# Seven products in place of eight for a part of the second feed-forward matrix, in an fp32 kernel of one core

## The reference

```python
def swiglu(x, w_in, w_out):
    gu = x @ w_in
    g, u = gu[..., :D_FF], gu[..., D_FF:]
    return (jax.nn.silu(g) * u) @ w_out
...
x = layer_norm(ALPHA * x + 0.5 * swiglu(x, ffn_w_in[l, 0], ffn_w_out[l, 0]), ln_g[l, 0], ln_b[l, 0])
...
    h = h + (jax.nn.silu(g_ff) * u_ff) @ w_ffn_out[l]
```

## Time and profile before

| | |
|---|---|
| time, median of 3 runs | 3251.34 us (3250.98 to 3256.97) |
| profiled execution | 3251.48 us, of which span from first to last instruction 3249.7 us |
| TensorE matmuls | 24214, busy 3157.5 us (97%) |
| VectorE | busy 2143.2 us (66%) |
| ScalarE | busy 1535.2 us (47%) |
| HBM read | 325.69 MB, 101 GB/s over the span |
| granted TensorE clock, mean | 0.994 |

### The profile page before, as it was taken

One profiled execution on the slowest core, in us unless ns is written; L12 is line 12 of the kernel. 1 busy time (PEld: TensorE's weight loads), 2 busy tenths in 40 slices (PEclk: granted clock), 3 DMA queues, 4 the chain that ended last, 5 costly groups with the idle time before them and its releaser, 6 DMA issues. The chain is left out here.

```text
span 3249.7 us, 58922 instructions
## 1 busy us (share of the span) xinstructions
PE 3157.5 (97%) x24214; PEld 2863.2 (88%) x24214; DVE 2143.2 (66%) x3383; ACT 1535.2 (47%) x2651; POOL 137.5 (4%) x144
## 2 busy tenths in 40 slices
PE   9999999999999999999999988999999989999999
PEld 9998998999889988779998877879998867789997
DVE  7875544788577856448875766557874665667863
ACT  4553444355435543644553544444554444444553
POOL 0000111000000001000000100000000000000000
PEclk9999999999999999999999999999999999999999
DMA  4343222234323332112433221113332211123332
GB/s 180 143 141 110 95 72 90 76 136 148 117 88 127 134 121 93 53 66 88 143 134 123 86 72 60 37 63 117 131 142 97 99 66 53 41 83 119 141 126 72
DMA packets 104523, 331.73 MB, mean 102 GB/s; under 512 B 11264, under 2 KB 16640, under 8 KB 104256
## 3 DMA queue, kind: packets, MB, share of 16 engines
q1 hardware_dynamic: 104256, 327.96, 28.7%
HBM read 325.69 MB, written 2.23 MB: 101 GB/s over the span
## 5 line engine op out<-in xcount | busy, mean ns | idle before, releaser
L222 DVE TENSOR_TENSOR wlo<-raw,whi 128x1024 fp32r<-128x1024 f32 x319 | 387.7, 1224 | 433.3 <-ACT whi L214 432.6
L214 ACT ACTIVATE whi<-raw 128x1024 fp32r<-128x1024 f32 x319 | 334.2, 1055 | 386.4 <-PE ps L379 333.5
L803 PE MATMUL ps<-tz,whi 128*128 128x256 f32 x1728 | 477.6, 276 | 3.4 <-ACT tmp L975 3.4
L804 PE MATMUL ps<-tz,whi 128*128 128x256 f32 x1728 | 477.1, 276 | 0.0
L805 PE MATMUL ps<-tz,wlo 128*128 128x256 f32 x1728 | 477.1, 276 | 0.0
L241 PE MATMUL ps<-xh,whi 128*128 128x256 f32 x1424 | 410.3, 288 | 18.4 <-DVE wlo L222 11.1
L377 PE MATMUL ps<-whi,tz 128*128 128x512 f32 x1056 | 412.1, 390 | 0.0
L379 PE MATMUL ps<-whi,tz 128*128 128x512 f32 x1056 | 411.0, 389 | 0.0
L378 PE MATMUL ps<-wlo,tz 128*128 128x512 f32 x1056 | 410.9, 389 | 0.0
L243 PE MATMUL ps<-xh,wlo 128*128 128x256 f32 x1424 | 397.9, 279 | 0.0
L242 PE MATMUL ps<-xl,whi 128*128 128x256 f32 x1424 | 397.7, 279 | 0.0
(11 more groups left out here) (348 smaller groups left out, 6509.2 us busy)
## 6 DMA issues: line engine op xcount, KB each, us to landing
raw<-in_w SPq DMA_DIRECT2D x535, 512.0 KB, 3.7
fb<-in_w SPq DMA_DIRECT2D x108, 256.0 KB, 2.5
rows<-in_row SPq DMA_DIRECT2D x15, 512.0 KB, 4.6
xr<-in_xt SPq DMA_DIRECT2D x4, 512.0 KB, 6.6
xr<-in_x SPq DMA_DIRECT2D x1, 2048.0 KB, 7.4
mn<-bounds SPq DMA_DIRECT2D x8, 256.0 KB, 4.6
out<-tmp SPq DMA_DIRECT2D x4, 256.0 KB, 3.5
out<-rows SPq DMA_DIRECT2D x4, 256.0 KB, 2.3
```

Source lines behind the costliest of these rows:

```text
L214: a.activation(self.whi[u % NW][:, :], self.raw[u % NRAW][:, :], COPY).then_inc(*self.up("whi", u))
L222: v.tensor_tensor(self.wlo[u % NW][:, :], self.raw[u % NRAW][:, :], f32(self.whi[u % NW][:, :]), SUB).then_inc(*self.up("wlo", u))
L803: t.matmul(out, fh[:, sl], xh[:, k, :], start=first and k == 0, stop=False, skip_group_check=not first)
L804: t.matmul(out, fh[:, sl], xl[:, k, :], start=False, stop=False, skip_group_check=not first)
```

## The change

In each feed-forward layer row blocks 6 to 13 (`PRE` = 6, `POST` = 14) of the second matrix are multiplied by the seven-product scheme. The quarters are: row blocks 6 to 9 and 10 to 13, the two 256-column halves of a column half, and the even and the odd token tiles. Products are made for each pair p of token tiles (0, 1 and 2, 3).

The order on TensorE becomes (`out_t`): row blocks 0 to 5 of half 0, then of half 1; seven products for half 0; row blocks 14 to 21 of half 0; seven products for half 1; row blocks 14 to 21 of half 1. The sums over row blocks 0 to 5 are taken out of PSUM and added to the residual (`part_v`), and the rest is added at the end by `add_v`. A row block's matmuls have 256 columns in place of 512 (`rows_t`). The activations of a row block are split once: high parts into `tz`, low parts into `hr`, which takes the place of `hf` in memory. The forms of the activations (`HAND`, `hand_a`, `hand_sum_v`, `hand_low_v`) are made once, in the place of `xh` and `xl` (`xx`), `tz` and `hr`. The forms of the weights (`out_sum_v`, `out_hi_a`, `out_lo_v`) are made for each half: four units of quarters give seven forms, which take the buffers `whi` and `wlo` in turn. Two of the sums lie in `fb` and `es`, two are made in place in `raw`. The stream of weights is reordered to match. The places in memory are shifted by padding.

```diff
-LINE = 16
+LINE = 32
+PRE = 6
+POST = 14
+PAIRS = (POST - PRE) // 2
+OUT_ORDER = (1, 5, 2, 6, 3, 7, 4)
...
+        self.v0 = u0 + 2 * KF
+        self.nm = nm.start(self.v0, KF)
+        for h in range(2):
+            v = self.first(h)
+            for i in range(4):
+                c.freed[v + 4 + i] = "prod", s, "out", h, OUT_ORDER[4 + i if i < 3 else 3], 1
+                c.read[v + i] = "flo", s, "out", h, (0, 5, 6, 4)[i]
...
+    def first(self, h):
+        return self.v0 + PRE + h * (KF - PRE) // 2
...
+    def out_from(self, h, f):
+
+        one, two = self.fb[:, :], self.es[:, 0:2, :].rearrange("p a n -> p (a n)")
+        return (self.out_raw(h, 0), one, self.out_raw(h, 2), two, self.out_raw(h, 3), self.out_raw(h, 1), self.out_raw(h, 2))[f]
...
+    def rows_t(self, t, h, k, i, first=False, last=False, event=None):
...
+        for e in range(2):
+            cs = slice(e * HT, e * HT + HT)
+            t.matmul(b[:, cs], hh[:, sl], wh[:, cs], start=first and e == 0, stop=False, skip_group_check=k >= POST)
+            t.matmul(b[:, cs], hh[:, sl], wl[:, cs], start=False, stop=False, skip_group_check=k >= POST)
+            ins = t.matmul(b[:, cs], hl[:, sl], wh[:, cs], start=False, stop=last and e == 1, skip_group_check=k >= POST)
...
+    def out_product(self, t, h, n, p, f):
...
+        for q in range(PAIRS):
+            x, cs = 2 * q + p, slice(q * HT, q * HT + HT)
+            t.matmul(out, fh[:, x, :], wh[:, cs], start=first and q == 0, stop=False, skip_group_check=not first)
+            if n == 1 and q == 0:
+                t.matmul(self.abe(h, p, r)[:, HT:T], fh[:, x, :], wh[:, cs], start=False, stop=False, skip_group_check=True)
+            t.matmul(out, fh[:, x, :], wl[:, cs], start=False, stop=False, skip_group_check=not first)
+            ins = t.matmul(out, fl[:, x, :], wh[:, cs], start=False, stop=q == PAIRS - 1, skip_group_check=not first)
...
+    def seven_out_t(self, t, h):
+        c, s, n = self.c, self.s, self.nm.n
+        for f, x in enumerate(OUT_ORDER):
+            if x == 4:
+                t.wait_ge(*c.at("g2", s, "out", h, 0))
+                for k in (POST, POST + 1):
+                    if k == POST:
+                        t.wait_ge(*c.at("wlo", self.unit_of(h, k)))
+                    t.wait_ge(*c.at("hl", s, k))
+                    self.rows_t(t, h, k, 0)
+            t.wait_ge(*c.at("flo", s, "out", h, f))
...
+            for p in range(2):
+                if x == 1 and h == 0:
+                    t.wait_ge(*c.at("part", n, 0, 2 * p))
+                elif x == 5:
+                    t.wait_ge(*(c.at("res", n, 0, 2 * p) if h else c.at("part", n, 1, 2 * p)))
...
+                self.out_product(t, h, x, p, f)
...
+    def out_hi_a(self, a, h, f):
+
+        c, s, u = self.c, self.s, self.first(h)
+        a.wait_ge(*(c.at("gemm", "unit", u - NW + f) if f < NW else c.at("prod", s, "out", h, OUT_ORDER[f - NW], 1)))
...
+    def out_a(self, a):
...
+        for h in range(2):
+            for f in range(4):
+                self.out_hi_a(a, h, f)
+                if h == 0 and f == 1:
+                    self.split_a(a, POST + 2, POST + 3)
+            self.out_seed_a(a, h, 0)
+            self.out_seed_a(a, h, 1)
+            self.out_hi_a(a, h, 4)
+            self.out_e5_a(a, h, 0)
+            self.out_e5_a(a, h, 1)
+            self.out_hi_a(a, h, 5)
+            self.out_hi_a(a, h, 6)
+            self.out_u2c_a(a, h, 0)
+            self.out_u2c_a(a, h, 1)
+            if h == 0:
+                self.split_a(a, POST + 4, POST + 5)
...
+            u = self.first(h) + 4
+            c.one_hi(a, u + 3)
+            c.one_hi(a, u)
+            c.one_hi(a, u + 1)
+            if h == 0:
+                self.split_a(a, POST + 6, POST + 7)
+            c.one_hi(a, u + 2)
...
+    def out_v(self, v):
...
+        c.one_lo(v, units[3])
+        c.one_lo(v, units[2])
+        self.hand_sum_v(v, "S1")
+        self.hand_sum_v(v, "S3")
+        self.hand_sum_v(v, "S2")
+        c.one_lo(v, units[4])
+        self.hand_sum_v(v, "S4")
+        self.hand_low_v(v, "A11", "A12")
+        c.one_lo(v, units[5])
+        self.hand_low_v(v, "S1")
+        for i in range(4):
+            self.part_v(v, 0, i)
+        self.out_sum_v(v, 0, 1)
+        self.out_lo_v(v, 0, 0)
+        self.hand_low_v(v, "S2")
+        self.out_sum_v(v, 0, 2)
+        self.out_lo_v(v, 0, 1)
+        self.hand_low_v(v, "S4")
+        self.out_sum_v(v, 0, 3)
+        self.out_lo_v(v, 0, 2)
+        self.out_sum_v(v, 0, 4)
+        self.hand_low_v(v, "S3", "A22")
+        for i in (0, 2, 1, 3):
+            self.part_v(v, 1, i)
+        for h in range(2):
+            self.out_lo_v(v, h, 3)
+            if h == 0:
+                self.split_v(v, POST, POST + 1)
+            self.out_lo_v(v, h, 4)
+            if h == 0:
+                self.split_v(v, POST + 2, POST + 3)
+            self.out_lo_v(v, h, 5)
+            self.out_lo_v(v, h, 6)
+            u = self.first(h) + 4
+            if h == 0:
+                self.split_v(v, POST + 4, POST + 5)
+            c.one_lo(v, u + 3)
+            self.out_g2_v(v, h, 0)
+            self.out_g2_v(v, h, 1)
+            c.one_lo(v, u)
+            self.out_u2_v(v, h, 0)
+            self.out_u2_v(v, h, 1)
+            c.one_lo(v, u + 1)
...
+            c.one_lo(v, u + 2)
```

More of the change, by code:

```diff
@@ L210, in hi, with one_hi @@
             u = self.nhi
[L211 to L214, removed]
+            self.one_hi(a, u)
             self.nhi += 1
+    def one_hi(self, a, u):
+        a.wait_ge(*self.at(f"raw{u % NRAW}", u))
+        if u >= NW:
+            a.wait_ge(*self.at(*self.freed.get(u, ("gemm", "unit", u - NW))))
+        a.activation(self.whi[u % NW][:, :], self.raw[u % NRAW][:, :], COPY).then_inc(*self.up("whi", u))
     def lo(self, v, upto):
@@ L329, in __init__, with start @@
         self.banks = (first, 4 - first)
-    def start(self, u0, k, feed=None):
-        self.u0, self.k, self.feed = u0, k, feed
+    def start(self, u0, k):
+        self.u0, self.k = u0, k
         self.end = u0 + k
@@ L683, in scalar @@
             c.hi(a, u + AHEAD)
-            if self.feed:
-                self.feed.split_a(a, 2 * (u - u0) + 4)
             if u0 + K // 2 < u <= u0 + K // 2 + 4:
                 self.square_a(a, 0, u - u0 - K // 2 - 1)
[L688 to L691, removed]
-        if not self.kind:
-            for i in range(4):
-                self.copy_a(a, 0, i)
         c.hi(a, self.end - 1)
@@ new lines, in out_lo_v, with part_v @@
+    def out_lo_v(self, v, h, f):
+        c, s = self.c, self.s
+        hi, lo = self.out_form(h, f)
+        v.wait_ge(*c.at("fhi", s, "out", h, f))
+        v.tensor_tensor(lo[:, :], self.out_from(h, f), f32(hi[:, :]), SUB).then_inc(*c.up("flo", s, "out", h, f))
+    def part_v(self, v, h, i):
+        c, nm = self.c, self.nm
+        v.wait_ge(*c.at("gemm", "part", nm.n, h, i))
+        if nm.n == 0 and h == i == 0:
+            v.wait_ge(*c.at("xrin"))
+        x = c.xr[:, i, 4 * P * h:4 * P * h + 4 * P]
+        v.scalar_tensor_tensor(out=x, in0=nm.bank(h, i), scalar=nm.by, in1=x, op0=MULT, op1=ADD).then_inc(*c.up("part", nm.n, h, i))
@@ new lines, in out_u2_v @@
+    def out_u2_v(self, v, h, p):
+        c, s = self.c, self.s
+        v.wait_ge(*c.at("prod", s, "out", h, 7, p))
+        v.wait_ge(*c.at("e5", s, "out", h, p))
+        b = self.abe(h, p, 1)
+        v.tensor_tensor(b[:, HT:T], b[:, 0:HT], c.tmp[p][:, HT:T], ADD).then_inc(*c.up("u2", s, "out", h, p))
+    def out_a(self, a):
+        c, v0 = self.c, self.v0
+        units = [self.unit_of(h, k) for h in range(2) for k in range(0, PRE, 2)]
+        self.split_a(a, 4, 5)
+        c.one_hi(a, units[3])
+        c.one_hi(a, units[2])
+        self.hand_a(a, "A11")
+        c.one_hi(a, units[4])
+        self.hand_a(a, "A12")
+        self.hand_a(a, "A22")
+        self.hand_a(a, "S1")
+        c.one_hi(a, units[5])
+        self.hand_a(a, "S3")
+        self.hand_a(a, "S2")
+        self.hand_a(a, "S4")
+        self.split_a(a, POST, POST + 1)
+        for h in range(2):
[14 more added lines that the diff above has]
+                self.split_a(a, POST + 4, POST + 5)
+            else:
+                for i in range(4):
+                    self.nm.square_a(a, 0, i)
+            u = self.first(h) + 4
[5 more added lines that the diff above has]
+            c.one_hi(a, u + 2)
+        c.nhi = self.nm.end
+        self.nm.finish_a(a)
```

321 lines of the change are left out of this document (269 added, 52 removed).

## The result

The changed kernel takes **3318.5 us** (median of 4 executions, 3304.5 to 3325.75) against 3251.2 us for the kernel before (4 executions, 3248.1 to 3257.0): ratio **1.020**, 95% interval 1.0162 to 1.0238. The forecast was 3291 us with a range of 3262 to 3312. The direction was right, the size was not: the kernel lost 67 us where 40 were forecast.

A forecast was written before the change was run, and what follows sets the result against it. The count of matmul columns on TensorE was taken to set the time in the rewritten stretch. 3251.3 - 29.9 (columns) + 51.0 (waits) + 18.6 (clock) = 3291 us, range 3262 to 3312.

The forecast's parts named there:

- Columns removed, -29.9 us: Second matrix, first feed-forward layers: 1012 units of 256 columns against 1056, 4.99 us a layer saved, 29.9 in all.
- Waits of the fetches, +51: TensorE waits after product 7 and before product 5 for late weights and sums: 8.5 us a layer, before the columns' gain.
- The landing, taken as 4.4 us: Time for the late weight unit u+3, fetched behind another, to arrive: 4.4 us, against 3.0 for a single fetch.
- The wait of 0.8 us before product 5: First half: product 5 waits for the second half's first `part` on VectorE, 0.8 us a layer.
- Clock, +18.6: The two TensorE pauses a layer lower the granted clock behind them, 1.7 us each time: 3.1 us a layer.
- The chance: Probability that a TensorE pause is followed by the lower clock: 0.95 for 4.2 us, 0.85 for 3.4 us.
- Two at 113.3 ns are one at 226.7 ns, so I take nothing: Second matrix: halving matmuls from 512 to 256 columns costs no time.
- The fixed cost per matmul: Skill page's 2.5 ns per matmul: 484 more matmuls a layer, estimated 1.2 us, 7 in all; not used.
- The one with 117.5 ns: Rival: second-matrix products and narrow rows run at 117.5 ns, 14 us more, 3305 us; chance 0.12 shared with longer low clock.
- The clock stays low for longer: Rival: 3.4 us lost at each TensorE pause, 41 us, giving 3313 us; chance 0.12 shared with slow narrow matmuls.
- the case that held them: Outcome class of slow narrow matmuls or longer low clock, 3303 to 3320 us, chance 0.12.
- The covered fetch: Rival: unit u+3 is in its buffer when ScalarE comes to it, so the kernel gets faster, 3226 us; chance 0.13.

The follow-up runs named there:

- e_ow_hh: Changed kernel with needed weight steps first, second-matrix rows at 512 columns, and only the activations' high parts moved to 112 bytes modulo 128: 3238.0 us, ratio 0.9947.
- e_order: Changed kernel with ScalarE and VectorE making the needed weight forms of unit u before those of the late unit u+3: 3247.1 us, ratio 0.9978.
- e_fetch: Changed kernel with only the fetch order altered, unit u+3 issued right behind unit u: 3245.0 us, ratio 0.998.
- e_fill: Changed kernel with 30 and 20 unused 256-column matmuls per layer where TensorE would pause in the first and second half: 3292.5 us, ratio 1.012.
- b_narrow: Kernel before with only its second matrix at 256 columns per matmul instead of 512, old memory places: 3293.3 us, ratio 1.012.
- b_layout: Kernel before with only the changed kernel's padding ahead of the feed-forward tiles, second matrix still at 512 columns: 3274.4 us, ratio 1.0057.
- b_nar_lay: Kernel before with its second matrix at 256 columns per matmul and the changed kernel's padding: 3278.5 us, ratio 1.0074.
- e_wide: Changed kernel with the row matmuls outside the seven products at 512 columns again: 3311.4 us, ratio 1.0185.
- e_ow_pad: Changed kernel with needed weight steps first, rows at 512 columns, and 64 bytes less padding ahead of the activations' tiles: 3270.4 us, ratio 1.0043.

## Why the prediction was wrong, step by step

- *Columns removed, -29.9 us: right.* The counts agree (27118 matmuls). No version got all of it back: e_ow_hh, with the pauses gone, is some 17 us below the kernel before in the median, and its trace still has wider spacing than that kernel's.
- *Waits of the fetches, +51: right in cause and place, a little large.* Forecast 4.2 and 3.4 us a layer in one piece each, 45.6 us in all; measured 4.1 to 4.9, and 2.6 to 3.6, 45.0 us together. That these agree so well is in part luck. The landing, taken as 4.4 us, took 5.5 to 6.4 in the first halves and 4.1 to 5.1 in the second; against that, TensorE reached the end of product 7 later (in the first layer the 458 matmuls up to there took 1.8 us more than at 113.3 ns each), and its wait was shorter by as much. Each link of the chain is in the trace, and two independent edits of it (e_order, e_fetch) take it away. The wait of 0.8 us before product 5 did not appear: no idle time is shown at its lines. That is most of the difference of 6.
- *Clock, +18.6: too small.* Measured +27 by the granted clock and 26 by e_fill. The chance was right, eleven pauses of twelve lowered the clock, but each was dearer: 27 us over eleven is 2.5 us each, where I had taken 1.7 from the one pause of the kernel before. Behind the pause that ends at 289.07 the first 5 us alone have 0.55, a loss of 2.25 us. The Trainium skill ("TensorE: Matmul & The Clock Gate", "HAM oscillation — how this bites in real kernels") has idle gaps put TensorE back to 1.2 GHz. The runs agree: 237 ns a matmul behind a pause, and a granted clock of 0.994 and 0.995 where the pause was filled (e_fill) or gone (e_order).
- *"Two at 113.3 ns are one at 226.7 ns, so I take nothing": this step failed.* It put the spacing of the matmuls at nothing, for the halved width and, without a word, for the new places in memory. Spacing cost +35 us in the profiled pair and +22 us in the second profiled execution of the changed kernel. I had seen 117.5 ns in 24 products and priced it as a rival at 14 us, for the new work alone. What the runs put in its place: width and place act together. b_narrow pays 40 us for the halving in the old places; b_layout pays 20 us for the padding, with no instruction changed; in the new places, which are the changed kernel's, the halving adds little (b_nar_lay against b_layout 5 us, the changed kernel against e_wide 7). And a wide level can hold for a whole first matrix, which the change does not touch. The padding lines were in the diff, and I gave them no price. The rows from which I argued, long runs of products at 113.3 ns, showed the spacing of those operands in those places, not of a width. The fixed cost per matmul that I cited from the Trainium skill (same page, "Wait — 56ns, not 53.3ns?") does not describe it either: in the kernel before, the narrow products and the wide rows cost the same per column (113.4 and 227.2), and the same narrow instructions take 117.9 or 120.0 by their place.
- *The rivals.* The one with 117.5 ns had the right sign and 3305 us; rows and products of the second matrix came at 116.3 and 116.6 ns in the mean. What it lacked is the rest of the kernel: about half of the 35 us lies in the first matrix and the projections. "The clock stays low for longer" was partly right, 2.5 us a pause where it had 3.4. Both came together, and the case that held them had a chance of 0.12. The covered fetch is what e_fetch makes of the kernel, and it gives 3245, not 3226; its trace, of its slowest execution, has some 50 us of excess.

With the measured sizes the sum is 3251.3 - 29.9 + 45 + 27 + 35 = 3328, against 3325.75 in that execution and 3318.5 in the median. For the second profiled execution, with +22 for spacing and 3 us more of idle time, it is 3318, and 3318.1 was measured.

**Shown:** the order of the weight steps and the late fetch as cause of the pauses; the pauses as cause of the clock loss; the padding as cause of a wider spacing in the kernel before; the halving as a cost of 40 us in the old places. **Open:** how the +35 us of the changed kernel divide between width and place, since no version of it ran at 113.3 ns throughout; which measure of a place counts and why it costs what it does, why the rows of e_ow_hh stop at 231.2 ns, and what decides in an execution whether a layer's first matrix runs at 113.3 or 117.8.

## What to carry to other kernels

When work is issued ahead, look at what stands behind it in the same engine's program: an early step on late data is worse than a late step. Treat a change of tile places, padding included, as a change of TensorE's time, and measure it alone, without the change it came with; check the operands that were not meant to move. Measure the spacing of matmuls over long runs, by line and by layer, since neither their durations nor the busy share show a 4% wider one.

## What the runs showed of the hardware

- Matmuls of 256 columns in this kernel come at 113.3, 117.8 or 120.0 ns, and of 512 columns at 226.7, about 231 or 233.3, at a granted clock of 1.00. A level holds over hundreds to some 1500 matmuls.
- Padding that moves the stationary activations by 64 bytes modulo 128 (and other tiles with them) changed it in both directions: narrow rows 119.9 to 117.6 (b_nar_lay), wide rows 227.2 to 232.5 (b_layout). The better place for one width was the worse one for the other.
- With the moving operand moved by 64 bytes, the matmuls that read it went from 114.2 to about 118.8 ns (e_ow_pad); those of the same stages that read a tile in its old place were at 113.7 to 115.0.
- A fetch of 512 KB issued 0.4 us behind another took 5.5 to 6.4 us to land in the first halves of the six layers and 4.1 to 5.1 in the second.
- Pauses of TensorE of 2.7 to 4.9 us were followed by a granted clock of 0.50 to 0.69 over the next 5 us, eleven times of twelve. Matmuls that fill them and do nothing useful kept the mean clock at 0.994 in place of 0.986 and saved 26 us (e_fill).
